# A fused two-block kernel: the recurrence's units in 27 steps instead of 35

## The reference

```python
def step(S, inp):
    r_t, w_t, k_t, v_t, kk_t, a_t = inp
    sa = jnp.einsum('bhvk,bhk->bhv', S, -kk_t)
    S = S * w_t[:, :, None, :] + sa[..., None] * (kk_t * a_t)[:, :, None, :] + v_t[..., None] * k_t[:, :, None, :]
    return S, jnp.einsum('bhvk,bhk->bhv', S, r_t)
...
_, y = lax.scan(step, S0, (tm(r), tm(w), tm(k), tm(v), tm(kk), tm(a)))
```

## Time and profile before

| | us |
|---|---|
| median of three runs (1937.18 to 1940.73) | 1939.88 |
| the profiled execution, its time | 1937.42 |
| its span on the core | 1935.6 |
| TensorE busy in it | 1861.6 (96%), 16241 matmuls |
| VectorE busy | 950.9 (49%) |
| ScalarE busy | 803.3 (42%) |
| GpSimd busy | 412.3 (21%) |
| mean granted TensorE clock | 0.994 |

### The profile page before, as it was taken

The page is one execution under the profiler, slowest core; times in us unless marked ns, Lnnn a source line. Parts: engine busy times, 40 slices in busy tenths (PEclk is TensorE's granted clock), DMA queues, the critical chain, the costliest instruction groups (busy, mean ns, idle before and its releaser), DMA issues. The chain is left out here.

```text
span 1935.6 us, 38827 instructions
## 1 busy us (share of the span) xinstructions
PE 1861.6 (96%) x16241; PEld 1523.9 (79%) x16241; DVE 950.9 (49%) x2072; ACT 803.3 (42%) x1773; POOL 412.3 (21%) x416
## 2 busy tenths in 40 slices
PE   6999999999997999989999999999999999999998
PEld 6997766888885999867777777777777786667898
DVE  5677766143346154035564444444444456775514
ACT  5346666243345133224333333333333256555421
POOL 4550000111114232312222222222222201001221
PEclk9999999999999999999999999999999999999999
DMA  5152310423331423331112221211122230005432
GB/s 185 45 181 78 83 33 1 129 84 112 117 115 56 153 79 95 105 101 58 58 59 61 67 69 58 61 59 59 58 74 60 75 104 12 1 1 183 161 125 88
DMA packets 148854, 159.92 MB, mean 83 GB/s; under 512 B 14948, under 2 KB 132008, under 8 KB 148680
## 3 DMA queue, kind: packets, MB, share of 16 engines
q1 hardware_dynamic: 148456, 156.44, 25.5%
q0 software_dynamic: 224, 0.99, 0.2%
HBM read 110.53 MB, written 52.62 MB: 84 GB/s over the span
## 5 line engine op out<-in xcount | busy, mean ns | idle before, releaser
L684 PE MATMUL ps<-t,t 128*128 128x256 f32 (+2 forms) x1392 | 432.9, 311 | 9.1 <-DVE t L2147 4.2
L2726 POOL TENSOR_TENSOR t<-t,t 128x512 fp32r<-128x512 f32 x183 | 238.0, 1315 | 909.3 <-ACT t L1349 893.8
L685 PE MATMUL ps<-t,t 128*128 128x256 f32 (+2 forms) x1392 | 426.2, 306 | 0.0
L686 PE MATMUL ps<-t,t 128*128 128x256 f32 (+2 forms) x1392 | 426.1, 306 | 0.0
L956 PE MATMUL ps<-t,t 128*128 128x512 f32 (+2 forms) x720 | 298.4, 414 | 1.0 <-ACT t L1625 1.0
L684 PEld LDWEIGHTS ps<-t,t 128*128 128x128 f32 x1392 | 267.5, 192 | 27.1 <-issue 13.7
L686 PEld LDWEIGHTS ps<-t,t 128*128 128x128 f32 x1392 | 267.3, 192 | 10.9
L685 PEld LDWEIGHTS ps<-t,t 128*128 128x128 f32 x1392 | 267.6, 192 | 10.2 <-issue 0.2
L958 PE MATMUL ps<-t,t 128*128 128x512 f32 (+2 forms) x720 | 268.8, 373 | 0.0
L957 PE MATMUL ps<-t,t 128*128 128x512 f32 (+2 forms) x720 | 268.6, 373 | 0.0
L1349 ACT ACTIVATE t<-t 128x512 fp32r<-128x512 f32 x182 | 107.9, 623 | 140.0 <-DMA t<-in_w_in 84.4
(11 more groups left out here) (265 smaller groups left out, 2964.5 us busy)
## 6 DMA issues: line engine op xcount, KB each, us to landing
t<-in_w_in SPq DMA_DIRECT2D x53, 512.0 KB, 6.0
zgate_spill<-t SPq DMA_DIRECT2D x20, 512.0 KB, 3.2
tile_bias<-t SPq DMA_DIRECT2D x16, 576.0 KB
t<-tile_bias SPq DMA_DIRECT2D x8, 1152.0 KB, 6.4
t<-in_x SPq DMA_DIRECT2D x16, 512.0 KB, 9.8
t<-zgate_spill SPq DMA_DIRECT2D x16, 512.0 KB, 3.5
feat_spill<-t SPq DMA_DIRECT2D x13, 512.0 KB, 3.2
tile_bias<-band_bias SPq DMA_DIRECT2D x48, 128.0 KB
```

The costliest lines, as they stand in the source:

```text
L684: e.matmul(dst, lh, rh, start=k == 0, stop=False)
L685: e.matmul(dst, lh, rl, start=False, stop=False)
L686: m = e.matmul(dst, ll, rh, start=False, stop=k == n - 1)
L2726: e.tensor_tensor(WLO[wslot(b)][:, o], WST[:, o], WHI[wslot(b)][:, o].bitcast(F), ALU.subtract).then_inc(w_lo.sem, w_lo.up((b, p)))
```

## The change

A unit has 27 steps. The transposes a and v go into the two halves of one bank, b and k into those of another; all four and the bonus product are one step (7). Then: 8 the first Gram product; 9 n2 and n2t (in the halves of one bank, both read by VectorE) and the second Gram product; 10 n4, n4t, d2; 11 x, n8t, d3; 12 d4; 13 f and z; 14 to 16 z0 to z2; 17 mt and q together; 18 g and y together; 19 to 22 the chain; 23 centering, 24 sums, 25 spread, 26 the last scaling. Whoever reads a shared bank first waits for the last product in it. `OFFSET` becomes 14, the steps' costs are set anew, and the remaining `late` steps (a few transposes for the next stage) draw dense pieces too. GpSimd's and the DMA queue's programs get the same steps. No product and no elementwise instruction is added or dropped; n2's copy moves from ScalarE to VectorE.

```diff
@@ -547,7 +547,7 @@
...
-        STAGE_US, NAT_US, INV_US, CHAIN_US, NORM_US, LOAD_US, OFFSET = 0.94, 0.61, 0.57, 0.67, 0.54, 8, 18
+        STAGE_US, NAT_US, GRAM_US, INV_US, PLAN_US, CHAIN_US, NORM_US, LOAD_US, OFFSET = 0.94, 1.1, 0.8, 0.6, 0.7, 0.67, 0.54, 8, 14
@@ -583,7 +583,7 @@
...
-                    pass
+                    self.fill(0.7)
@@ -1016,8 +1016,11 @@
...
-                def turn(name, src, *ready):
-                    ps = mine(("turn", name), (prep_a, (u, "turn", name)))
+                def turn(two, name, src, *ready):
+                    if name == two[0]:
+                        mine(("turn", two), (prep_a, (u, "turn", two[1])))
+                    ps = psum((u, ("turn", two)))[:, 256 * two.index(name):256 * two.index(name) + 256]
@@ -1025,16 +1028,14 @@
...
-                turn("a", None, prep_v[u, "a0"])
-                turn("v", S.FV[:, 1:TU + 1], prep_v[u, "v1"])
-                yield NAT_US
-                turn("b", CU, prep_v[u, "bh"])
-                turn("k", SG, prep_v[u, "kh"])
-                yield NAT_US
+                turn("av", "a", None, prep_v[u, "a0"])
+                turn("av", "v", S.FV[:, 1:TU + 1], prep_v[u, "v1"])
...
+                turn("bk", "b", CU, prep_v[u, "bh"])
+                turn("bk", "k", SG, prep_v[u, "kh"])
@@ -1050,15 +1051,13 @@
...
-                for s, done in ((0, "not"), (1, "rkt")):
-                    ps = mine_two(("gram", s), (gram_v, (u, done)))
+                def gram_pair(s):
+                    ps = mine_two(("gram", s), (gram_v, (u, "rkt" if s else "not")))
...
-                    yield INV_US
-                def blocks(key, lhs, rhs, *emptied):
-                    ps = mine(key, *emptied)
+                def blocks(key, ps, lhs, rhs):
@@ -1068,32 +1067,32 @@
...
+                gram_pair(0)
+                yield GRAM_US
+                ps = mine("n2 both", (inv_v, (u, "n2t")))
                 w.wait_ge(*gram_v[u, "ndt"])
-                blocks("n2", whole(NDT), whole(ND), (inv_a, (u, "n2")))
-                blocks("n2t", whole(ND), whole(NDT), (inv_v, (u, "n2t")))
-                yield INV_US
+                blocks("n2", ps[:, 0:256], whole(NDT), whole(ND))
+                blocks("n2t", ps[:, 256:512], whole(ND), whole(NDT))
+                gram_pair(1)
+                yield GRAM_US
+                w.wait_ge(*inv_v[u, "n2t"])
+                blocks("n4", mine("n4", (inv_a, (u, "n4"))), whole(B4), whole(B3))
+                blocks("n4t", mine("n4t", (inv_v, (u, "n4t"))), whole(B3), whole(B4))
+                w.wait_ge(*prep_p[u, "d1"])
+                blocks("d2", mine("d2", (inv_v, (u, "d2"))), whole(B4), whole(B5))
+                yield GRAM_US
                 w.wait_ge(*gram_v[u, "rkt"])
                 w.wait_ge(*prep_a[u, "turn", "v"])
-                blocks("x", whole(AKT), lambda pq, x: VNN[pq, x % MP, 64 * (x // MP):64 * (x // MP) + 64], (inv_a, (u, "x")))
-                yield INV_US
-                w.wait_ge(*inv_a[u, "n2"])
-                w.wait_ge(*inv_v[u, "n2t"])
-                blocks("n4", whole(B4), whole(B3), (inv_a, (u, "n4")))
-                blocks("n4t", whole(B3), whole(B4), (inv_v, (u, "n4t")))
-                yield INV_US
-                w.wait_ge(*prep_p[u, "d1"])
-                blocks("d2", whole(B4), whole(B5), (inv_v, (u, "d2")))
-                yield INV_US
+                blocks("x", mine("x", (inv_a, (u, "x"))), whole(AKT), lambda pq, x: VNN[pq, x % MP, 64 * (x // MP):64 * (x // MP) + 64])
                 w.wait_ge(*inv_a[u, "n4"])
                 w.wait_ge(*inv_v[u, "n4t"])
-                blocks("n8t", whole(ND), whole(NDT), (inv_a, (u, "n8t")))
-                yield INV_US
+                blocks("n8t", mine("n8t", (inv_a, (u, "n8t"))), whole(ND), whole(NDT))
                 w.wait_ge(*inv_v[u, "d2"])
-                blocks("d3", whole(NDT), whole(B6), (inv_v, (u, "d3")))
-                yield INV_US
+                blocks("d3", mine("d3", (inv_v, (u, "d3"))), whole(NDT), whole(B6))
+                yield GRAM_US
                 w.wait_ge(*inv_a[u, "n8t"])
                 w.wait_ge(*inv_v[u, "d3"])
-                blocks("d4", whole(B3), whole(B5), (inv_v, (u, "d4", 1)))
+                blocks("d4", mine("d4", (inv_v, (u, "d4", 1))), whole(B3), whole(B5))
@@ -1119,20 +1118,21 @@
...
-                for name, terms, emptier in (("mt", [(W_, H_(BHN))], plan_v), ("g", [(H_(BHN), U_), (H_(KHN), H_(VNN))], plan_a),
-                                             ("q", [(W_, G_(ARB))], plan_v), ("y", [(U_, G_(ARB)), (H_(VNN), G_(RKT))], plan_a)):
-                    ps = mine_two(name, (emptier, (u, name)))
+                for two, emptied, terms_of in (("mq", (plan_v, (u, "q")), (("mt", [(W_, H_(BHN))]), ("q", [(W_, G_(ARB))]))),
+                                               ("gy", (plan_a, (u, "y")), (("g", [(H_(BHN), U_), (H_(KHN), H_(VNN))]), ("y", [(U_, G_(ARB)), (H_(VNN), G_(RKT))])))):
+                    ps = mine_two(two, emptied)
                     w.wait_ge(*inv_v[u, "z2"])
                     w.wait_ge(*prep_a[u, "turn", "k"])
-                    for m in range(MP):
-                        for pairs in (((0, 0), (1, 1)), ((0, 1), (1, 0))):
-                            for y, (l, r) in enumerate(terms):
-                                for x, q in pairs:
-                                    pq = slice(64 * q, 64 * q + 64)
-                                    i = e.matmul(ps[q][64 * x:64 * x + 64, 64 * m:64 * m + 64], l(x, pq, m), r(x, pq, m),
-                                                 start=y == 0, stop=y == len(terms) - 1)
-                    i.then_inc(plan_mm.sem, plan_mm.up((u, name)))
-                    yield INV_US
+                    for part, (name, terms) in enumerate(terms_of):
+                        for m in range(MP):
+                            o = slice(128 * part + 64 * m, 128 * part + 64 * m + 64)
+                            for pairs in (((0, 0), (1, 1)), ((0, 1), (1, 0))):
+                                for y, (l, r) in enumerate(terms):
+                                    for x, q in pairs:
+                                        pq = slice(64 * q, 64 * q + 64)
+                                        i = e.matmul(ps[q][64 * x:64 * x + 64, o], l(x, pq, m), r(x, pq, m), start=y == 0, stop=y == len(terms) - 1)
+                        i.then_inc(plan_mm.sem, plan_mm.up((u, name)))
+                    yield PLAN_US
@@ -1662,45 +1662,40 @@
...
-                    pv = psum((u, ("turn", name)))[:, 0:TU].rearrange("p (m c) -> p m c", c=128)
+                    two = "av" if name in "av" else "bk"
+                    pv = psum((u, ("turn", two)))[:, 256 * two.index(name):256 * two.index(name) + 256].rearrange("p (m c) -> p m c", c=128)
...
+                w.wait_ge(*turn_tr[u, "v"])
                 turn("a")
                 turn("v")
-                yield NAT_US
+                w.wait_ge(*turn_tr[u, "k"])
                 turn("b")
                 turn("k")
-                yield NAT_US
...
-                yield INV_US
-                yield INV_US
+                yield GRAM_US
+                yield GRAM_US
...
-                w.wait_ge(*prep_v[u, "bonus"])
-                w.wait_ge(*prep_p[u, "dg"])
-                blocks_out("n2", B3)
-                yield INV_US
-                blocks_out("x", ZA_[:, :, 64:128])
-                yield INV_US
...
-                yield INV_US
-                yield INV_US
+                yield GRAM_US
+                w.wait_ge(*inv_mm[u, "n4t"])
                 blocks_out("n8t", B3)
-                yield INV_US
-                yield INV_US
+                blocks_out("x", ZA_[:, :, 64:128])
+                yield GRAM_US
@@ -1711,12 +1706,12 @@
...
-                for name, dst in (("mt", None), ("g", S.GS), ("q", None), ("y", S.YL)):
-                    if dst is not None:
-                        w.wait_ge(*plan_mm[u, name])
-                        pv = psum_two(lambda q: (u, (name, q)), 0, 64 * MP).rearrange("p q (m c) -> p q m c", c=64)
-                        e.activation(dst[:, :, :].rearrange("p (m q) c -> p q m c", q=2), pv, ACT.Copy).then_inc(plan_a.sem, plan_a.up((u, name)))
-                    yield INV_US
+                yield PLAN_US
+                for part, (name, dst) in enumerate((("g", S.GS), ("y", S.YL))):
+                    w.wait_ge(*plan_mm[u, "y"])
+                    pv = psum_two(lambda q: (u, ("gy", q)), 64 * MP * part, 64 * MP).rearrange("p q (m c) -> p q m c", c=64)
+                    e.activation(dst[:, :, :].rearrange("p (m q) c -> p q m c", q=2), pv, ACT.Copy).then_inc(plan_a.sem, plan_a.up((u, name)))
+                yield PLAN_US
@@ -2392,7 +2385,7 @@
...
-                w.wait_ge(*prep_a[u, "turn", "k"])
+                w.wait_ge(*turn_tr[u, "k"])
@@ -2405,31 +2398,30 @@
...
-                yield INV_US
+                yield GRAM_US
+                def block(key, bank=None, first=0):
```

(34 more changed lines are left out.)

24 lines of the change are left out of this document (11 added, 13 removed).

## The result

The changed kernel takes 1934.43 us (median, 1931.66 to 1938.85) against 1939.40 for the kernel before beside it: 0.9976 of its time, 95% interval 0.9967 to 0.9986. It is 5.0 us faster where 17 were forecast; the direction is right, the size is not, and the time lies just above the range. The profiled execution has a span of 1931.9 us against 1935.6, so 3.7 less.

What follows compares the result with a forecast made beforehand. TensorE was taken as the bound, busy 701.0 of 719.0 us. Terms -20.7 - 4.0 + 6.3 - 1.5 + 1.0 + 1.0 + 1.0 = -16.9 gave 1920.5 us, as median 1923; 8-in-10 range 1912 to 1934.

Steps and rivals of the forecast that it cites:

- The bound, and the price of a run: TensorE bounds, busy 701.0 of 719.0 us; 61 fewer runs of 64 x 64 matmuls at 0.34 us, 20.7 us less.
- the 97%: Sign: the forecast is wrong as a whole if TensorE is busy for clearly less than 97% of the recurrence.
- Rival E: Joining products of different banks doesn't save entry and exit, so the 20.7 us is missing: 1943.7 us, chance 0.04.
- The bank wait that goes: The second Gram product no longer waits for VectorE's four copies from the first one's banks: 4.0 us less.
- The square: Flow 1's step 24 sums wait for ScalarE's square behind two copies: 0.9 us in 7 rounds, +6.3 us.
- the two entries: +6.3 us for flow 1's square; -1.5 us for flow 0's square, no longer behind flow 1's copy of x.
- The f copy and the start: ScalarE's late f copy in flow 1's step 13, +1.0 us; flow 0 alone for its first 13 steps, +1.0 us.
- Dense pieces moved: Some 61 dense pieces run after the recurrence, 42 us in all, gapless; the move costed at nothing.
- The turned step 7: Four transposes and bonus product beside VectorE's bo, bh, kh: taken as 0, bounds 0 and 0.2 us in 8 units.
- The end: Next stage's second weight waits for splits behind the last dense output; load starts later, +1.0 us, bounds 0 and 2.
- (C): Rival: more places like the square than were found give back half the gain: 1931 us, chance 0.12.
- (D): Rival: slower, TensorE waits for the second of VectorE's 48 pairs of copies; 1948 us at 0.52 each, chance 0.05.

Runs made afterwards that it cites:

- Cutting runs: Changed kernel with one dense piece of each unit moved between n4t and d2 of step 10, cutting a run of 48 in two: 1939.74 us, 1.0004.
- the late steps alone: Changed kernel with the late transposes two steps later and three dense pieces, not one, behind each closing step: 1935.24 us, 0.9981.
- the earlier weight: Changed kernel with the load of the next stage's first weight (key and value) asked for one block earlier: 1932.77 us, 0.9965.
- all repairs: Changed kernel with late steps later, GpSimd's last split before its end-of-recurrence wait, next stage's weight loaded earlier, x copied one step later: 1925.71 us, 0.993.
- the small splits: GpSimd's low-part subtraction on 16 of 512 columns, low parts wrong: changed kernel 1922.77 us, 0.9914; kernel before 1933.0 us, 0.9966.

## Why the prediction was right in direction and wrong in size

- **The bound, and the price of a run**: right. 61 runs fewer, as counted ahead (169 and 230), 21.4 us at 0.35 each against 20.7 forecast. TensorE's busy share is 96.5% of the recurrence, just under the 97% that the prediction had set as its sign. Cutting runs gave it back at 0.37 each. Rival E, that joining doesn't save, falls with the run of 48 and with that experiment.
- **The bank wait that goes**: right, 4.5 against 4.0.
- **The square**: the place and the mechanism are right, in all 7 rounds; the size was 0.9 a round and is 0.59: I put the two copies at 0.8 us, but the square begins 0.55 after the first of them (1098.81 to 1099.36), and TensorE would have been free 1.15 + 0.47 = 1.62 us after x began, not 1.55. Together the two entries were +4.8, and are +3.5.
- **The f copy and the start**: the f copy right, 0.9 in 6 waits (in front of L1101, for ScalarE's L1705) against 1.0. The start 1.0 too much: its wait is 4.6 as before.
- **Dense pieces moved**, costed at nothing: this is the step that failed. The gapless stretch behind the recurrence was read off of the kernel before, where nothing of the next stage was in the way. I noted that 6 pieces go beside the late steps and didn't ask what these steps do: power and scalings, in front of the transposes, are a chain of 7.0 us from 1488.99 to 1495.98, which before ran beside recurrence steps. The work that hid it moved away. Cost 5.2 us, forecast 0.
- **The turned step 7**, taken as 0 with bounds 0 and 1.6: the three instructions of VectorE were put at 0.45 each, from rows in which GpSimd did nothing. Beside a split one lasts 1.5. The wait is 2.6 us by the waits' view, above the bound. With it belongs a term that the sum doesn't have at all: GpSimd's splits were weighed only as transfers that must keep pace, not as something that slows VectorE and stands in front of the spread. That is some 5.2 us, 2 of them in the late chain.
- **The end**, +1.0 with bounds 0 and 2: the wait is 4.06 against 1.83, +2.2, and behind it the matmuls run at the lower clock, 0.32 us apart and not 0.18 for some three us, which is the other 1.5. From the next stage's first matmul to the end of the span 3.8 us are given back. The mechanism was named, its size was not: I bounded the load's delay by the splits, and the load itself is asked for later because the first weight lands late.

By the terms: forecast -16.9; the late chain +5.2, the splits without it about +3, the end +2.8, the runs (-0.7), the bank wait (-0.5), the square (-1.3) and the start (-1.0) together -3.5; and of the small waits that the sum left out, the copy of z rose by 1.1 (L2432, 1.4 in 4 against 0.3) and those of the plan's products went (-2.1). That gives -10.4, and the medians say -5.0. Some 5 us remain that no row and no experiment here assigns; the other matmuls' 1.3 us is a part. The two measured terms are known to 3 and 5 us only, so the remainder may be in part their error, and it stays open.

Of the rivals, (C) was nearest: more places like the square. Most of what was found is of another kind than it supposed, a chain without cover and an engine that slows another. (D), VectorE's pairs of copies, didn't come: TensorE waits nowhere for the copies of n2t, n4t, d2 and d3 (L2409, L2418, L2420, L2423), and 0.2 us for that of d4 (L2430). The Trainium skill's rule on emptying PSUM (TensorEngine Tiling (Array Packing), PSUM Bottleneck) is therefore not what limits this case; VectorE is busy for 344 of 663 us.

## What to carry to other kernels

When work is moved away from a place, list what it was hiding there, down to the small chains of the next stage, and price each chain from its first to its last instruction against what is left beside it. A count of saved entries (here runs of one tile shape) is worth its price only if the order on the other engines stays as it was: an alignment of two flows with 14 runs fewer was 14 us slower. When a repair of one wait shows nothing, look for the next wait in its place before the theory is dropped: here the late steps alone gave nothing, and with one line more 5.2 us.

## What the runs showed of the hardware

- A run of 64 x 64 matmuls among full-width ones costs 0.34 to 0.37 us for its entry and exit together, in runs of 16, 32 and 48, and whether it writes one bank or three. The Trainium skill says that changing the tiling mode drains TensorE (TensorEngine Tiling (Array Packing), Key Properties); it gives no figure, and the trace agrees with the rule.
- A VectorE instruction over 256 columns that reads two operands in SBUF can last 1.2 to 1.5 us instead of 0.4 when a GpSimd instruction over 512 columns (1.28 to 1.5 us) runs beside it; with GpSimd's made short, none is over 1.1 us. Each of the 12 long ones in the changed kernel ends 0.28 us after a split of GpSimd's, or 0.15 us if it is a scaling with a column of scalars, as if it had waited for it. The 15 instructions over 256 columns with an operand in PSUM that begin during a split keep their 0.41 to 0.43 us. The Trainium skill has the rule (SBUF — State Buffer, SBUF: two separate sides): the two engines share a port pair by exclusive lock, and the other one blocks for the whole instruction. The trace agrees, VectorE's scalings with a column of scalars (L2516, 1.34 us) included.
- After TensorE had waited for 4.1 us at 1492 to 1496, and again for 4.06 us before 1553.70, matmuls took 0.63 and 0.52 us where they take 0.40 and 0.34: the lower of the two levels, 1.2 GHz, for some of the ten microseconds, which is what the granted 0.83 of both stretches means. The second such stretch costs 1.5 us on top of the wait. The length of the wait alone doesn't say whether this happens: behind the 2.6 us of the earlier weight the clock stayed at 1.00, and with all repairs, behind a wait of the same 2.6 us, it fell to 0.51; with the small splits it fell to 0.50 behind 2.1 us (the changed kernel, 1485.5 to 1488.5), and to 0.52 behind 1.8 us (the kernel before, 1555 to 1558), but stayed at 1.00 behind 3.0 us (the same run, 843.5 to 850).
